# Modulation vectors in a three-layer transformer kernel: four blocks of partial sums transposed into one PSUM bank and summed by VectorE, instead of one-column matmuls after each unit

## The chip, the cores and the metric

The kernel runs on one core of one Trainium2 chip. The metric is the device time of one execution in microseconds (us), the median of the runs shown. The profile is of one execution on the same core. TensorE is called PE in the rows, VectorE DVE, ScalarE ACT, GpSimd POOL, SyncE SP.

## What is computed

512 tokens with 1024 channels go through a first block (retention with four heads, dilated attention in three groups, a gated merge, a squared-ReLU feed-forward) and then through two layers of a second block, the first of which also carries 256 context tokens. Every norm is modulated and every branch gated by vectors that depend on a conditioning vector `c` alone:

```python
mod = jax.nn.silu(c) @ w_ada[l] + b_ada[l]          # (1024) @ (1024 x 6144)
sh1, sc1, g1, sh2, sc2, g2 = jnp.split(mod, 6, axis=-1)
h = modulate(rms_norm(x, norm1_g[l]), sh1, sc1)     # h * (1 + scale) + shift
x = x + g1[:, None, :] * token_mixer(h, ...)
h = modulate(rms_norm(x, norm2_g[l]), sh2, sc2)
x = x + g2[:, None, :] * squared_relu_mlp(h, w_ff1[l], w_ff2[l])
# second block, l = 0, 1: the same six vectors from c_2, and six more from c_ctx_2 for the context,
# both times the same matrix ada_w_2[l]
```

The change concerns how `silu(c) @ w_ada` is summed. Each of the three matrices has 1024 rows and 6144 columns, which are 48 blocks ("chunks") of 128 columns.

## The kernel before, in words

**Units.** All large products run in 244 units of up to 256 weight columns. SyncE loads a unit's weights into `raw`, ScalarE copies them to `w_hi` (`hi`), VectorE subtracts to get `w_lo` (`lo`, L1582), and TensorE does three matmuls for each 128 rows (`product`, L539 to L542) in `gemm`. The weights have two buffers, so `hi` and `lo` of unit n+2 can start only when unit n has been multiplied. A unit with 1024 rows is called a long one here, a unit with 512 rows (the second matrix of a feed-forward) a short one. In the layer with context a unit also multiplies the context tokens. A feed-forward is a head of 2 units, a hardware loop of 3 bodies of 12 units (2 long, 4 short, 2 long, 4 short; units 0 to 11 of a body), and a tail of 10 units (2 long, 8 short; units 0 to 9).

**Modulation vectors.** The first 16 chunks of the first matrix are done ahead of everything. The other 128 are spread over the program. For each, GpSimd (`chunk`, L2188) waits for its DMA, multiplies the 128x1024 block by the vector (L2195), adds eight slices to four, two and one (L2197, L2199, L2201) and leaves a 128x128 block of partial sums in `ada_acc`: its columns have still to be summed over the 128 partitions. The 96 chunks of the second block's matrices are done for two vectors, one after the other, since `c_2` and `c_ctx_2` meet the same weights. After that GpSimd issues the DMA for the chunk after next (L2186). `ada_acc` has two halves, and `ada_raw` two buffers.

**One step for each chunk.** `ada_mm_step` (L663) on TensorE waits until GpSimd has summed the chunk (`ada_sum`) and until VectorE has read the chunk before (`ada_evac`), and multiplies `ada_acc` by a column of ones: one matmul of one column for a one-vector chunk, two for a two-vector chunk. VectorE adds the bias and writes the result to `mod1` (L1625) or `mod2` (L1635). GpSimd may start chunk a when chunk a-2 has been multiplied. In the retention heads eight steps are written out for each head; elsewhere the table `ADA` says how many steps stand behind each unit, in `ada_steps` on TensorE and `ada_outs` on VectorE. The three engines run through the program in their written order, so a step that isn't ready stops TensorE there, and a VectorE instruction that waits for a step stops the `lo` of later units behind it.

## Time and profile before

| | us |
|---|---|
| median of 3 runs (lowest, highest) | 3363.69 (3362.53, 3374.6) |
| the profiled execution, span | 3362.5 |
| TensorE busy in it | 3102.6 (92%) |
| VectorE busy | 1717.3 (51%) |
| ScalarE busy | 1180.7 (35%) |
| GpSimd busy | 1340.9 (40%) |

The span runs from the first to the last instruction, and the median lies 1.2 us above it. Start times below count from the span's start. Busy shares are means over the whole program; what a place waits for is read from the idle time in brackets in the timeline.

### The profile page before, as it was taken

What the parts mean: (1) busy time and instruction counts of PE and PEld (TensorE: products, weight loads), DVE (VectorE), ACT (ScalarE), POOL (GpSimd) and SP (SyncE); (2) the same over time, 40 slices, a digit from 0 to 9 for tenths busy, and PEclk for the clock granted to TensorE, in tenths of its full rate; (3) what the DMA queues carried; (4) which work ended last, traced back from release to release, by engine and by line L of the source; (5) the groups of instructions that cost most, each with busy time, mean ns of one, the idle gap of its engine ahead of it and who ended that gap; (6) DMA issues with size and microseconds to landing.
All of it is one profiled execution on the core that took longest, in us unless ns stands there. A gap on an engine that the chain in (4) does not pass through costs nothing.

```text
span 3362.5 us, 42485 instructions
## 1 busy us (share of the span) xinstructions
PE 3102.6 (92%) x16079; PEld 2615.0 (78%) x16079; DVE 1717.3 (51%) x1792; ACT 1180.7 (35%) x1683; POOL 1340.9 (40%) x1044
## 2 busy tenths in 40 slices
PE   5799999999999899989988899999999988989998
PEld 4677777798987688868977778887887878868886
DVE  4563464424146766763177457655554437544444
ACT  2232233213133333343245433322324326434433
POOL 2445336753536677734610056777770000000000
PEclk7899999999999899999998999999999999999999
DMA  7333332433323334432230022322222221013331
GB/s 264 113 113 97 115 106 94 141 96 94 100 65 125 92 116 125 131 95 69 82 82 1 13 76 63 101 88 89 88 88 70 75 73 28 26 57 97 97 100 63
DMA packets 257779, 303.30 MB, mean 90 GB/s; under 512 B 23340, under 2 KB 229564, under 8 KB 257629
## 3 DMA queue, kind: packets, MB, share of 16 engines
q1 hardware_dynamic: 234716, 224.43, 21.5%
q0 software_dynamic: 19456, 72.00, 7.1%
q10 hardware_dynamic: 3456, 4.72, 0.5%
q8 instruction: 112, 1.84, 0.2%
q14 instruction: 39, 0.31, 0.0%
HBM read 291.95 MB, written 9.18 MB: 90 GB/s over the span
## 4 chain that ended last, share of the span: by engine, by line
PE 31%; POOLq 31%; issue 27%; DVE 4%; DVEq 1%; POOL 1%; SPq 1%; ACT 1%; DMA 0%; ACTq 0%
POOLq L2196 12%; POOLq L2198 9%; PE psum L540 9%; PE psum L541 8%; PE psum L542 8%; POOLq L2200 6%; POOLq L2204 4%; POOL ada_raw L2186 1%; PE psum L873 1%; PE psum L713 1%; DVE w_lo L1582 1%; PE psum L883 1%; SPq L431 1%; PE psum L619 1%; PE psum L698 1%
## 5 line engine op out<-in xcount | busy, mean ns | idle before, releaser
L2195 POOL TENSOR_TENSOR ada_prod<-ada_raw,csil 128x1024 f32<-128x1024 f32 x224 | 453.7, 2026 | 777.8 <-PE psum L669 757.6
L540 PE MATMUL psum<-hs_hi,w_hi 128*128 128x512 f32 x1632 | 653.7, 401 | 60.9 <-DVE hs_lo L1574 35.4
L1582 DVE TENSOR_TENSOR w_lo<-raw,w_hi 128x2048 fp32r<-128x2048 f32 (+1 forms) x244 | 536.9, 2200 | 315.1 <-ACT w_hi L1062 246.6
L541 PE MATMUL psum<-hs_hi,w_lo 128*128 128x512 f32 x1632 | 644.2, 395 | 0.0
L542 PE MATMUL psum<-hs_lo,w_hi 128*128 128x512 f32 x1632 | 643.6, 394 | 0.0
L2197 POOL TENSOR_TENSOR ada_prod<-ada_prod 128x512 f32<-128x512 f32 x224 | 372.0, 1661 | 195.0 <-issue 181.2
L540 PEld LDWEIGHTS psum<-hs_hi,w_hi 128*128 128x128 f32 x1632 | 312.3, 191 | 130.4 <-issue 44.0
L542 PEld LDWEIGHTS psum<-hs_lo,w_hi 128*128 128x128 f32 x1632 | 311.7, 191 | 67.4
L541 PEld LDWEIGHTS psum<-hs_hi,w_lo 128*128 128x128 f32 x1632 | 312.6, 192 | 63.1
L540 PE MATMUL psum<-mid_hi,w_hi 128*128 128x512 f32 x768 | 303.0, 395 | 5.5 <-DVE w_lo L1582 5.4
L542 PE MATMUL psum<-mid_lo,w_hi 128*128 128x512 f32 x768 | 299.4, 390 | 0.0
L541 PE MATMUL psum<-mid_hi,w_lo 128*128 128x512 f32 x768 | 298.9, 389 | 0.0
L1841 DVE TENSOR_TENSOR X<-X,y_t 128x512 f32<-128x512 f32 x208 | 202.3, 983 | 167.1 <-ACT y_t L1324 166.9
L1825 DVE TENSOR_TENSOR r_t<-r_t 128x512 f32<-128x512 f32 x112 | 122.8, 1099 | 313.3 <-ACT r_t L1307 313.2
L1324 ACT ACTIVATE y_t<-psum,mod 128x512 f32<-128x512 f32 x208 | 143.0, 690 | 335.4 <-PE psum L542 315.1
L2199 POOL TENSOR_TENSOR ada_prod<-ada_prod 128x256 f32<-128x256 f32 x224 | 237.1, 1059 | 31.9
L1307 ACT ACTIVATE r_t<-psum 128x512 f32<-128x512 f32 x112 | 66.9, 598 | 450.8 <-PE psum L542 447.2
L540 PE MATMUL psum<-w_hi,hs_hi 128*128 128x256 f32 x704 | 214.8, 305 | 0.0
L541 PE MATMUL psum<-w_hi,hs_lo 128*128 128x256 f32 x704 | 213.7, 304 | 0.0
L542 PE MATMUL psum<-w_lo,hs_hi 128*128 128x256 f32 x704 | 213.7, 303 | 0.0
L1070 ACT CAST w_hi<-raw 128x2048 fp32r<-128x2048 f32 (+1 forms) x138 | 190.6, 1381 | 0.0
L1062 ACT CAST w_hi<-raw 128x2048 fp32r<-128x2048 f32 (+1 forms) x106 | 174.4, 1645 | 13.3 <-issue 8.9
(330 smaller groups left out, 5728.6 us busy)
## 6 DMA issues: line engine op xcount, KB each, us to landing
raw<-in_w_in SPq DMA_DIRECT2D x56, 1024.0 KB, 5.1
ada_raw<-in_ada_w POOLq DMA_DIRECT2D x96, 512.0 KB, 4.7
raw<-in_w_ff SPq DMA_DIRECT2D x48, 1024.0 KB, 5.5
raw<-in_w_ff SPq DMA_DIRECT2D x96, 512.0 KB, 3.4
ada_raw<-in_w_ada POOLq DMA_DIRECT2D x32, 512.0 KB, 4.6
raw<-in_w_in SPq DMA_DIRECT2D x24, 512.0 KB, 5.1
ada<-in_w_ada SPq DMA_DIRECT2D x4, 2048.0 KB, 23.9
raw<-in_w_ret_out SPq DMA_DIRECT2D x16, 512.0 KB, 3.4
```

What stands on the lines that cost most here:

```text
L540: pe.matmul(dst, lhi, rhi, start=start, stop=False)
L541: pe.matmul(dst, llo, rhi, start=False, stop=False)
L542: return pe.matmul(dst, lhi, rlo, start=False, stop=stop)
L1070: act.copy(w_hi[n0_ % 2][:, 0:kt], raw[n0_ % 2][:, 0:kt]).then_inc(hi_done, 1)
L1582: dve.tensor_tensor(w_lo[par][:, 0:kt], raw[par][:, 0:kt], w_hi[par][:, 0:kt].bitcast(F32), ALU.subtract).then_inc(lo_done, 1)
L1841: dve.tensor_tensor(X[:, q, :], X[:, q, :], y_t[r_][:], ALU.add).then_inc(y_free, 1)
L2195: pool.tensor_tensor(ada_prod[:], ada_raw[par][:], bass.AP(c_.tensor, c_.offset, [*c_.ap, [0, P]]), ALU.mult)
L2196: pool.drain()
L2197: pool.tensor_tensor(ada_prod[:, 0:4], ada_prod[:, 0:4], ada_prod[:, 4:8], ALU.add)
L2198: pool.drain()
L2199: pool.tensor_tensor(ada_prod[:, 0:2], ada_prod[:, 0:2], ada_prod[:, 2:4], ALU.add)
L2200: pool.drain()
```

## The change

Four blocks of partial sums now make a set: four one-vector chunks, or two two-vector chunks. `ada_acc` has two halves of four blocks. TensorE does one **turn** for each set (`ada_turn`): four transposes of 128x128 into the four quarters of one PSUM bank, where the sum over partitions has become a sum along the free dimension. VectorE reduces the whole bank to four columns (`ada_red`) with one `tensor_reduce` and adds the bias, with one instruction for the first matrix and two for the others. There are 56 turns (8 + 48), where there were 128 steps. GpSimd computes the same blocks in the same order with the same instructions and DMAs, but waits once for each set: set s starts when turn s-2 is done. In the heads two turns for each head are left, behind the second unit and at the head's end; the table `ADA` is written anew, so that in the tail of the feed-forward with context (`ff_tail_0`) there are now five turns, behind units 1, 3, 5, 7 and 9, and none at the end of its loop body. Some buffers move to make room, and `gn_rstd` becomes the same memory as `gn_std`.

```diff
-ADA = {"gate_a": [1, 1, 0, 1], "ret_out": [0, 1, 0, 0], "att0": [1, 1, 1, 1, 0, 1, 1, 1, 0], "att1": [1, 1, 1, 1, 0, 1, 1, 1, 0],
-       "gate_b": [1, 1, 0, 1], "att_out": [0, 1, 0, 0], "w_o": [1, 1, 1, 1],
-       "ff_head": [1, 1], "ff_body": [1, 0, 0, 1, 0, 1, 0, 1, 0, 1, 0, 1], "ff_tail": [1, 0, 0, 0, 1, 0, 0, 0, 0, 0],
-       "w_in_0": [1] * 9, "w_out_0": [1] * 4, "ff_head_0": [1, 1], "ff_body_0": [1, 1, 0, 1, 1, 1, 1, 1, 0, 1, 1, 1],
-       "ff_tail_0": [1, 0, 1, 0, 1, 0, 0, 0, 0, 0]}
+ADA = {"gate_a": [0, 1, 0, 1], "ret_out": [0, 0, 0, 1], "att0": [0, 1, 0, 1, 0, 1, 0, 1, 0], "att1": [0, 1, 0, 1, 0, 1, 0, 1, 0],
+       "gate_b": [0, 1, 0, 1], "att_out": [0, 0, 0, 1], "w_o": [0, 1, 0, 1],
+       "ff_head": [0, 0], "ff_body": [0, 1, 0, 0, 0, 0, 0, 1, 0, 0, 0, 0], "ff_tail": [0, 1, 0, 0, 0, 1, 0, 0, 0, 0],
+       "w_in_0": [0, 1, 0, 1, 0, 1, 0, 1, 0], "w_out_0": [0, 1, 0, 1], "ff_head_0": [0, 1],
+       "ff_body_0": [0, 1, 0, 0, 1, 0, 0, 1, 0, 0, 1, 0], "ff_tail_0": [0, 1, 0, 1, 0, 1, 0, 1, 0, 1]}
...
-            def ada_mm_step(a, vecs=1, bank_=C1):
+            def ada_turn(a, bank_=C1):
 
                 pe.wait_ge(ada_sum, a + 1)
                 if not (isinstance(a, int) and a == 0):
                     pe.wait_ge(ada_evac, a)
-                for v in range(vecs):
-                    mm = pe.matmul(bank_[:, v:v + 1], ada_acc[:, ada_par[0], v, :], ones_c[:, 0:1], start=True, stop=True)
+                for s_ in range(4):
+                    mm = pe.transpose(bank_[:, s_ * P:(s_ + 1) * P], ada_acc[:, ada_par[0], s_, :], ident[:])
                 ada_par[0] ^= 1
                 mm.then_inc(ada_mm, 1)
...
                 gemm(n, 0, hs_hi, hs_lo, ready=(hs_ready, lambda k: k + 1) if first else None)
-                ada_mm_step(8 * h)
                 gemm(n + 1, 1, hs_hi, hs_lo)
-                ada_mm_step(8 * h + 1)
+                ada_turn(2 * h)
...
-                ada_mm_step(8 * h + 2)
-                ada_mm_step(8 * h + 3)
                 gemm(n + 3, 1, hs_hi, hs_lo, tokens=tile_tok)
...
-                ada_mm_step(8 * h + 4)
-                ada_mm_step(8 * h + 5)
                 gemm(n + 4, 0, hs_hi, hs_lo)
...
-                ada_mm_step(8 * h + 6)
                 gemm(n + 5, 1, hs_hi, hs_lo)
...
-                ada_mm_step(8 * h + 7)
+                ada_turn(2 * h + 1)
...
             def ada_out(a):
 
                 dve.wait_ge(ada_mm, a + 1)
-                dve.tensor_tensor(mod1[:, bass.ds(16 + a, 1)], C1[:, 0:1], vec1[:, bass.ds(24 + a, 1)],
-                                  ALU.add).then_inc(ada_evac, 1)
+                dve.tensor_reduce(ada_red[:], C1[:].rearrange("p (s n) -> p s n", s=4), AX.X, ALU.add).then_inc(ada_evac, 1)
+                dve.drain()
+                dve.tensor_tensor(mod1[:, bass.ds(16 + 4 * a, 4)], ada_red[:], vec1[:, bass.ds(24 + 4 * a, 4)], ALU.add)
...
-                    j_ = a - (80 if l else 32)
-                    dve.tensor_scalar(mod2[l][:, :, bass.ds(j_, 1)], bank_[:, 0:2].rearrange("p (v o) -> p v o", o=1),
-                                      vec2[:, l, bass.ds(j_, 1)], None, ALU.add).then_inc(ada_evac, 1)
+                    dve.tensor_reduce(ada_red[:], bank_[:].rearrange("p (s n) -> p s n", s=4), AX.X, ALU.add).then_inc(ada_evac, 1)
+                    dve.drain()
+                    for c in range(2):
+                        j_ = 2 * (a - ADA_SETS - 24 * l) + c
+                        dve.tensor_scalar(mod2[l][:, :, bass.ds(j_, 1)], ada_red[:, 2 * c:2 * c + 2].rearrange("p (v o) -> p v o", o=1),
+                                          vec2[:, l, bass.ds(j_, 1)], None, ALU.add)
...
+            def sets_of_two(l, i, more=True):
+
+                for half in range(2):
+                    for k in range(2):
+                        chunk(k, 256 + 384 * l + 32 * i + 16 * half + 16, half, 2 * k, (0, 1),
+                              ADA_SETS - 1 + 24 * l + 2 * i + half if k == 0 else None, k == 1)
+                        if half == 0 or more:
+                            load_ada(wada2[l], 2 + 4 * i + 2 * half + k, k)
+                        elif l == 0:
+                            load_ada(wada2[1], k, k)
```

Three places show what moves. First TensorE at the end of the loop body of the feed-forward with context (`midc` and `hc` are the context's activations, `mid` and `hs` the tokens'). Before:

```order
L542 MATMUL psum<-midc_lo_138,w_hi_51 128x256
L665 REGISTER_ALU
L669 MATMUL psum<-ones_c,ada_acc 128x1 x2
L835 REGISTER_ALU
L835 COMPARE_AND_BRANCH
L540 MATMUL psum<-hs_hi,w_hi_52 128x512
```

And now:

```order
L545 MATMUL psum<-midc_hi_136,w_lo_53 128x256
L546 MATMUL psum<-midc_lo_138,w_hi_51 128x256
L833 REGISTER_ALU
L833 COMPARE_AND_BRANCH
L544 MATMUL psum<-hs_hi,w_hi_52 128x512
```

The step at the body's end is gone, and the last matmul of unit 11 stands directly ahead of the loop's branch and of unit 0 of the next body.

Second VectorE in a retention head, between the second weight-column unit and the rotation (`z_lo` is the low part of the head before, `w_lo` the low part of a unit's weights). Before:

```order
L1582 TENSOR_TENSOR w_lo_53<-raw_49,w_hi_51 128x1024
L1654 TENSOR_TENSOR z_lo<-ro,z_hi 128x2048
L1624 REGISTER_ALU
L1625 ISA
L1625 TENSOR_TENSOR mod_60<-psum,vec_59 128x1
L1581 REGISTER_ALU
L1582 TENSOR_TENSOR w_lo_54<-raw_50,w_hi_52 128x1024
```

And now:

```order
L1580 TENSOR_TENSOR w_lo_53<-raw_49,w_hi_51 128x1024
L1656 TENSOR_TENSOR z_lo<-ro,z_hi 128x2048
L1622 ISA
L1623 TENSOR_REDUCE ada_red<-psum 128x4
L1625 ISA
L1625 REGISTER_ALU
L1625 TENSOR_TENSOR mod_60<-ada_red,vec_59 128x4
L1579 REGISTER_ALU
L1580 TENSOR_TENSOR w_lo_54<-raw_50,w_hi_52 128x1024
```

A reduction and an addition of four columns stand where one addition of one column stood, ahead of the `w_lo` of a later unit; the other addition, ahead of the first `w_lo`, is gone.

Third VectorE at the end of the tail with context, where layer 1 of the second block begins (`scale` is its first scale vector, X and CX the residuals, `w_lo` of 2048 elements the units of layer 1). Before:

```order
L1841 TENSOR_TENSOR X<-X,y_t_142 128x512
L1841 TENSOR_TENSOR X<-X,y_t_143 128x512
L1844 TENSOR_TENSOR CX<-CX,y_t_144 128x512
L1582 TENSOR_TENSOR w_lo_54<-raw_50,w_hi_52 128x2048
L1841 TENSOR_TENSOR X<-X,y_t_142 128x512
L1841 TENSOR_TENSOR X<-X,y_t_143 128x512
L1844 TENSOR_TENSOR CX<-CX,y_t_144 128x512
L1909 SCALAR_TENSOR_TENSOR scale_73<-mod_1_72,vec_69 128x8 x2
L1582 TENSOR_TENSOR w_lo_53<-raw_49,w_hi_51 128x2048
```

And now:

```order
L1837 TENSOR_TENSOR X<-X,y_t_142 128x512
L1837 TENSOR_TENSOR X<-X,y_t_143 128x512
L1840 TENSOR_TENSOR CX<-CX,y_t_144 128x512
L1580 TENSOR_TENSOR w_lo_54<-raw_50,w_hi_52 128x2048
L1837 TENSOR_TENSOR X<-X,y_t_142 128x512
L1837 TENSOR_TENSOR X<-X,y_t_143 128x512
L1840 TENSOR_TENSOR CX<-CX,y_t_144 128x512
L1633 TENSOR_REDUCE ada_red<-psum 128x4
L1637 TENSOR_SCALAR mod_1_72<-ada_red,vec_69 128x2 x2
L1905 SCALAR_TENSOR_TENSOR scale_73<-mod_1_72,vec_69 128x8 x2
L1580 TENSOR_TENSOR w_lo_53<-raw_49,w_hi_51 128x2048
```

The residuals of units 8 and 9 had no modulation work behind them; now the reduction of the last turn stands between the last residual and the scales of the next layer.

## Rows read from the trace of the kernel before

**Rows 1.** The page of before, part 1: busy us, share of the span, instructions.

```profile
PE 3102.6 (92%) x16079; PEld 2615.0 (78%) x16079; DVE 1717.3 (51%) x1792; ACT 1180.7 (35%) x1683; POOL 1340.9 (40%) x1044
```

**Rows 2.** Line 669 from 2045 to 2592 us: idle time of PE and its weight loads before it.

```profile
  POOL ada_acc L2201: 30.8, 6
```

**Rows 3.** Timeline of PE at the first and last of three body ends: start, length, [idle].

```profile
2189.70 1.01 PE L669 MATMUL psum<-ones_c,ada_acc 128*128 128x1 f32 x4 [5.07 <-POOL ada_acc L2201]
2193.41 0.79 PE L540 MATMUL psum<-hs_hi,w_hi 128*128 128x512 f32 x1 [2.69 <-issue]
...
2487.21 0.95 PE L669 MATMUL psum<-ones_c,ada_acc 128*128 128x1 f32 x4 [5.02 <-POOL ada_acc L2201]
2488.02 0.77 PE L540 MATMUL psum<-hs_hi,w_hi 128*128 128x512 f32 x1
```

**Rows 4.** Windows behind those three waits: busy us, PEclk eighth.

```profile
2193.00:2203.00 10.00, 9.59 (x35) 7.78 (x35) 3.16 (x2) 0.60 (x1) 7.43 (x7) 0.79 0.26 90
2342.00:2352.00 10.00, 10.00 (x34) 7.95 (x34) 2.75 (x2) 0.60 (x1) 6.85 (x7) 0.73 0.20 65
2488.00:2498.00 10.00, 10.00 (x32) 7.99 (x33) 5.36 (x3) 0.60 (x1) 7.58 (x7) 0.69 0.35 105
```

**Rows 5.** GpSimd: its DMA issues from 2100 on, and parts of one chunk of two vectors.

```profile
L2186 POOL DMA_DIRECT2D ada_raw<-in_ada_w x27: 912/915/924, 2112.9 to 2501.5; - x27
...
2149.31 1.28 POOL L2197 TENSOR_TENSOR ada_prod<-ada_prod 128x512 f32<-128x512 f32 x1 [1.76 <-issue]
...
2158.62 0.73 POOL L2201 TENSOR_TENSOR ada_acc<-ada_prod 128x128 f32<-128x128 f32 x1
2160.17 0.92 POOL L2186 DMA_DIRECT2D ada_raw<-in_ada_w  x1 [0.82 <-issue]
```

**Rows 6.** Timeline of PE: a two-vector step, and four transposes (L923).

```profile
1695.19 0.60 PE L923 MATMUL psum<-ident,ws 128*128 128x128 f32 x4
1695.62 1.45 PE L931 MATMUL psum<-dft,u_f 128*128 128x512 f32 x3
...
2228.93 0.28 PE L542 MATMUL psum<-hc_lo,w_hi 128*128 128x256 f32 x1
2229.05 0.50 PE L669 MATMUL psum<-ones_c,ada_acc 128*128 128x1 f32 x4
2229.42 0.47 PE L540 MATMUL psum<-mid_hi,w_hi 128*128 128x512 f32 x1
```

**Rows 7.** One pair of steps in a retention head, and the waits of all eight.

```profile
142.78 0.28 PE L669 MATMUL psum<-ones_c,ada_acc 128*128 128x1 f32 x2
143.82 0.35 PE L669 MATMUL psum<-ones_c,ada_acc 128*128 128x1 f32 x2 [0.76 <-DVE mod L1625]
144.04 0.36 PE L540 MATMUL psum<-w_hi,hs_hi 128*128 128x256 f32 x1
...
  DVE mod L1625: 4.8, 8
```

**Rows 8.** Groups of VectorE by form: a reduction from PSUM, and the evacuation of a two-vector step.

```profile
L1635 DVE TENSOR_SCALAR mod<-psum,vec 128x2 f32<-128x2 f32 x48 | 10.4, 217 | 247.7 <-PE psum L669 247.7
...
L2006 DVE TENSOR_REDUCE dneg<-psum 128x2 f32<-128x512 f32 x8 | 5.5, 682 | 0.0
```

**Rows 9.** Timeline of VectorE in head 2: the same subtraction, twice.

```profile
335.25 1.23 DVE L1582 TENSOR_TENSOR w_lo<-raw,w_hi 128x1024 fp32r<-128x1024 f32 x1 [2.85 <-ACT w_hi L1070]
...
338.66 2.85 DVE L1582 TENSOR_TENSOR w_lo<-raw,w_hi 128x1024 fp32r<-128x1024 f32 x1
```

**Rows 10.** Waits of PE, heads 1 to 3 (first) and first feed-forward: us, times, longest.

```profile
PE psum L540 <- DVE w_lo L1582: 6.6, 3, 2.2
...
PE psum L540 <- DVE w_lo L1582: 5.7, 6, 1.5
```

**Rows 11.** The last eight units with context: window, and PE at their end.

```profile
2524.60:2592.30 67.70, 67.70 (x395) 59.99 (x393) 29.96 (x37) 27.53 (x42) 2.05 (x3) 1.00 0.25 78
...
2594.01 6.41 PE L619 MATMUL psum<-n_sq,mean_dm 128*128 128x512 f32 x13 [1.45 <-ACT n_sq L1102]
```

More of the change, by code:

```diff
@@ L101, in ada_starts @@
 def ada_starts():
-    start, a = {}, 32
+    start, a = {}, ADA_SETS
     for name in ADA:
@@ L2186, in load_ada, with chunk @@
                 pool.dma_start(ada_raw[par][:], w[:, :, bass.ds(chunk * P, P)]).then_inc(ada_in[par], 16)
-            def chunk(a, par, count, cond=(csil,), first=False):
+            def chunk(par, count, half, slot, cond=(csil,), free=None, last=False):
                 pool.wait_ge(ada_in[par], count)
-                if not first:
-                    pool.wait_ge(ada_mm, a - 1)
+                if free is not None:
+                    pool.wait_ge(ada_mm, free)
                 for v, c in enumerate(cond):
@@ L2231, in _, with sets_of_four @@
-            for par in range(2):
-                chunk(126 + par, par, 1024, (0, 1))
+            def sets_of_four(first_set, i, free):
+                for half in range(2):
+                    for k in range(4):
+                        chunk(k % 2, 64 * i + 32 * half + 16 * (k // 2) + 16, half, k,
+                              free=(free + half if k == 0 and free is not None else None), last=k == 3)
+                        load_ada(wada, 18 + 8 * i + 4 * half + k, k % 2)
+            sets_of_four(0, 0, None)
@@ new lines, in _ @@
+            with pool.Fori(1, 3) as i:
+                sets_of_four(2 * i, i, 2 * i - 1)
+            pool.wait_ge(v3_done, 1)
+            for half in range(2):
+                for k in range(4):
+                    chunk(k % 2, 192 + 32 * half + 16 * (k // 2) + 16, half, k, free=5 + half if k == 0 else None, last=k == 3)
+                    if half == 0 or k < 2:
+                        load_ada(wada, 42 + 4 * half + k, k % 2)
+                    else:
+                        load_ada(wada2[0], k - 2, k % 2)
@@ new lines, in sets_of_two @@
+            def sets_of_two(l, i, more=True):
+                for half in range(2):
+                    for k in range(2):
[5 more added lines that the diff above has]
+                            load_ada(wada2[1], k, k)
@@ L2235, in constants @@
+            for l in range(2):
+                with pool.Fori(0, 11) as i:
+                    sets_of_two(l, i)
+                sets_of_two(l, 11, False)
 def constants():
```

57 lines of the change are left out of this document (16 added, 41 removed).

## The prediction

> **What bounds the kernel now.** I read the page first: TensorE is busy for 92% of the span, the other engines for half of it or less [rows 1]. So TensorE's own time counts in most places, and an edit elsewhere counts where TensorE waits. Next came the waits of the modulation steps. From 2045 us on, in the feed-forward with context, TensorE and its weight loads stood idle for GpSimd's partial sums, 30.8 us in six entries, which are three waits seen by both [rows 2]. The timeline puts them at the ends of the three loop bodies [rows 3]: 5.07 us idle, then the step, then 2.69 us more before the next body's first matmul ("issue": nothing that the profile shows holds it; it comes after a wait right ahead of the loop's branch). The third wait has no branch back behind it, and no such gap. Behind each wait the windows show a mean granted clock of 0.79, 0.73 and 0.69 for 10 us [rows 4]; TensorE had idled some 5 to 9 us before it fell. Last I read GpSimd: from 2112.9 to 2501.5 us it issued 27 DMAs, one for each chunk, hence one two-vector chunk in 388.6 / 26 = 14.95 us, without a pause for TensorE [rows 5]. A body holds ten chunks, 149.5 us, while TensorE needs about 140 us for it: from 2193.41 to 2487.21, less the 5.02 us of the last wait and 8.8 us of the one between, are two bodies in 280 us [rows 3]. There GpSimd is the bound, and nowhere else for long.
>
> **What the change removes on TensorE.** A two-vector step costs 0.37 us: the matmul behind it starts 0.49 us after the one ahead of it, where 0.12 us is the usual spacing [rows 6]. There are 96. I leave out 13: three at the body ends (counted below), two in the tail (below), and eight which the timeline shows ahead of a wait for something else (weights, or the squares of a norm), where time saved is time waited. 83 x 0.37 = 30.7 us.
>
> A turn is four transposes. The trace has a group of four, 1695.19 to the next start at 1695.62, 0.43 us [rows 6]. From below it could cost 0.35 us (the next start doesn't wait for the end), from above four full lengths one after another, 4 x 0.27 = 1.1 us (0.27 is what the last of the four takes, 0.60 less 3 x 0.11). I take 0.43, the same operation in this kernel. Of the 48 later turns 4 are in the tail and 9 ahead of other waits: 35 x 0.43 = 15.1 us. Net gain 15.6 us.
>
> The Trainium skill, "TensorE: Matmul & The Clock Gate", Part 4, gives about 275 ns for a 128x128 bf16 transpose in a kernel's context. That would be 1.1 us for a turn, and 23 us less gain; the row above speaks for 0.11 us each in a row of four.
>
> **The retention heads.** Twice in each head two steps stand in a row, and the second waits for VectorE to have read the first: the pair at 142.78 costs 1.26 us, 0.76 of it waiting [rows 7]. All eight waits are 4.8 us, and the pairs' own time is 8 x 0.50: 8.8 us, all gone. Single steps and the one turn that isn't ahead of a wait give 0.2 us more. The other turns stand ahead of the wait for the group norm's chain, and cost TensorE nothing while it lasts. Gain 9.0 us.
>
> On VectorE a turn costs a reduction of 512 elements from PSUM, 0.68 us by the nearest row, a drain, and one or two small additions of 0.21 us [rows 8]: 1.0 us in the heads, 1.2 us later, where a step cost 0.2. Most of it lies beside idle time of VectorE. It doesn't behind the second unit of heads 1 to 3: `w_lo` of the coming units is queued behind it, and TensorE already waits three times for `w_lo` there, 6.6 us in all [rows 10]. 3 x 0.8 = 2.4 us lost. Also GpSimd will be ahead by a set of four and work through this stretch, where it now pauses. The same subtraction of 1024 elements took VectorE 1.23 us, and 2.85 us beside a multiplication of GpSimd's [rows 9]. I put 2 us on this (0 to 6). The Trainium skill, "GPSIMD Engine Reference", Key points, names such contention, for VectorE instructions with two SBUF inputs; the reduction, with one from PSUM, would be free of it. Net for the heads +4.6 us.
>
> **The first feed-forward.** The turns now stand behind units 1 and 7 of a body, and the reduction ahead of `w_lo` of unit 3 or 9, behind the squares of the hidden part. TensorE waits for `w_lo` six times in this feed-forward, 5.7 us [rows 10]. Four of the seven such places I count as lengthened by 1.0 us: 4 us lost (0 to 7). A turn moves no DMA queue: SyncE's loads keep their order, GpSimd's its own.
>
> **The body ends with context.** Four sets a body are eight chunks, 120 us against TensorE's 140, and no turn stands at the end. The waits go: 5.07 + 1.01 + 2.69 = 8.8 us, the second alike, the third 5.02 + 0.81 = 5.8 us [rows 3]: 23.4 us. The clock gives back 10 x (0.21 + 0.27 + 0.31) = 7.9 us, of which I take 7.5, since the first window begins 0.4 us before its matmuls [rows 4]. Gain 30.9 us.
>
> **What comes late instead: the tail with context.** The ten chunks that the bodies no longer take must come somewhere, and five turns now stand in the tail, behind units 1, 3, 5, 7 and 9. GpSimd can hold two sets at most, and set s starts when turn s-2 is done. Call the turn behind unit 1 time 0; it frees the half for the third of the five sets. A set's sum is ready 1.7 us before its second chunk's DMA is through (2159.35 to 2161.09) [rows 5], so the third set is ready at 0.8 + 29.9 - 1.7 = 29.0 us, in time for unit 5. The fourth starts at 30.7 and is ready at 58.9 us. TensorE is there earlier: the eight units behind time 0 take 67.7 us with two steps [rows 11], 67.0 without; six of them with two turns 51.1 us. It waits 7.8 us. The fifth set starts at 60.6; its first chunk ends 14.3 us later, its second, with no DMA behind or ahead of it, is ready after another 11.6 to 12 us [rows 5]: 86.9 us. TensorE is there at 59.3 + 16.8 = 76.1 us, and waits 10.8. The tail ends at 87.3 instead of 67.7 us. While TensorE waits VectorE is idle, and GpSimd quicker, 2 us off, and 1 us is hidden by the wait for the squares that stands behind it anyway (1.45 us [rows 11]): 17 us lost. A lower clock behind the first wait costs nothing, since GpSimd ends last. Behind the stopped turns VectorE's `w_lo` is held up as well, but TensorE needs it later. If a chunk takes 13.5 us, 9 us are lost; if 16, 23.
>
> **The sum.** 30.9 + 15.6 + 4.6 - 4 - 17 = 30.1 us gained, from the profile's span of 3362.5: 3332.4. The median of the runs is 1.2 us over it: 3334 us. A gain or loss of 0.5%, 17 us, is about what a measurement can tell from no change.
>
> **The rivals.**
> - *The tail costs little* (0.17): GpSimd, beside a VectorE with less to do, needs 13.5 us for a chunk. 8 us less lost, and the small losses in heads and feed-forward halve: 3322.
> - *VectorE holds up the units* (0.18): the reductions and GpSimd's steadier work lengthen waits for `w_lo` in the heads, behind the first gates, and at all seven places of the first feed-forward, or GpSimd is late once more in the dilated attention, where two chunks stand against two units. 12 us more lost: 3346. For it speaks that TensorE waits for `w_lo` already [rows 10], against it VectorE's 51% [rows 1].
> - *The transposes don't overlap* (0.05): 1.1 us a turn, 0.67 x 35 = 23 us: 3357.
> - *The other side, slower* (0.07): every turn stops VectorE's queue, for the evacuation has to wait for TensorE and then takes 1.2 us, and `hi` and `lo` of the next unit can't start before the last is multiplied. If 49 turns more than those counted pass 1.0 us each to TensorE, 49 us are lost and the time is 3383; it decides from 0.6 us each, where the gain is gone. Against it: behind a long unit with context VectorE has some 17 us for 3 us of work.
> - *The change doesn't do what it says* (0.03): GpSimd, with a chunk over 17.5 us, is the bound in the bodies still, and the waits move from their ends to units 1, 4, 7 and 10: about 3362.
>
> The forecast has 0.50, with a range of its own of 3327 to 3341. The likeliest is 3334. For 8 in 10 I cut the other side, the transposes, the lost change, and little below the cheap tail: 3319 to 3350. Faster by over 0.5% (below 3347): 0.50 + 0.17 + 0.12 of the held-up case = 0.79. Within: 0.06 + 0.05 + 0.03 = 0.14. Slower: 0.07.
>
> **What would show it.** The steps: 56 groups of four transposes, 0.43 us from start to start. The bodies: no wait for `ada_acc` in them, granted clock 1.00 at their start, 140 us each. The tail: two waits of TensorE for `ada_acc`, 6 to 11 us each, behind units 7 and 9. The heads: no wait for `mod`, and about 1 us more before the third short unit of heads 1 to 3. VectorE: a reduction of 0.68 us. I am wrong if the tail's waits are missing or double, if GpSimd's chunk moves far from 15 us, or if waits for `w_lo` grow by more than 10 us in all.

## The result, and the profile after it

The changed kernel takes 3417.76 us (median of 4 runs, 3413.49 to 3420.41), the kernel before on the same chip 3365.49 (4 runs). The ratio is 1.0151, with a 95% interval of 1.0136 to 1.0166: 1.5% slower. The forecast was 3334 us, so it missed by 84 us, and by sign.

The profiled execution took 3415.81 us, its span is 3413.7. This is the line of busy times on its page, to be set beside [rows 1]:

```profile
PE 3098.5 (91%) x15855; PEld 2581.5 (76%) x15855; DVE 1818.6 (53%) x1824; ACT 1180.5 (35%) x1683; POOL 1345.4 (39%) x1044
```

TensorE is busy for only 4 us less, where the light kernels below, a pair without most of GpSimd's arithmetic, differ by 24.5 us (3071.8 and 3047.3). Most of the other 20 us is a lower granted clock: its mean is 0.954 of full speed against 0.958 before, and 0.4% of 3100 us is 13 us (an estimate). In the light kernels it is 0.969 and 0.970. GpSimd has the same work. VectorE has 101 us more. The waits of TensorE over the whole span (us in all, times, longest) say what that does:

```profile
PE psum L544 <- DVE w_lo L1580: 79.8, 29, 9.1
PE psum L544 <- DVE hs_lo L1572: 44.0, 15, 11.1
...
PE psum L673 <- POOL ada_acc L2197: 12.4, 2, 7.3
```

In the kernel before the same view has 37.9 us in 20 waits for `w_lo`, 35.4 in 6 for `hs_lo` and 16.0 in 4 for `ada_acc`. So the waits for GpSimd became fewer, as the change set out to do, and those for VectorE grew by 50 us. The groups of VectorE by form (count, busy us, mean ns) show what is new there:

```profile
L1580 DVE TENSOR_TENSOR w_lo<-raw,w_hi 128x1024 fp32r<-128x1024 f32 x116 | 164.5, 1418 | 38.0 <-ACT w_hi L1060 19.8 <-ACT w_hi L1068 17.9
...
L1633 DVE TENSOR_REDUCE ada_red<-psum 128x4 f32<-128x512 f32 x48 | 32.8, 683 | 155.7 <-PE psum L673 155.7
...
L1637 DVE TENSOR_SCALAR mod<-ada_red,vec 128x2 f32<-128x2 f32 x60 | 31.1, 561 | 2.9
L1637 DVE TENSOR_SCALAR mod<-ada_red,vec 128x2 f32 x36 | 27.0, 791 | 5.7 <-issue 5.7
...
L1625 DVE TENSOR_TENSOR mod<-ada_red,vec 128x4 f32 x6 | 4.5, 744 | 1.9 <-issue 1.9
```

The reduction takes what [rows 8] said, 0.68 us. The small additions do not: in these groups they average 0.56 to 0.79 us in place of 0.22.

**Where the time went.** A table of stages, each from the first matmul of its first unit to that of the next stage, parts the two traces (the last columns are of experiments below). "Context" is the layer with context.

| Stage, us | before | changed | light before | light changed | e14 |
|---|---|---|---|---|---|
| four retention heads | 462.3 | 488.9 | 450.1 | 437.6 | 458.9 |
| gate_a, ret_out | 77.0 | 77.0 | 67.4 | 67.3 | 73.4 |
| attention, both passes | 332.3 | 335.4 | 328.9 | 326.8 | 336.4 |
| gate_b, att_out, w_o | 145.9 | 143.8 | 130.6 | 129.7 | 144.6 |
| first feed-forward | 408.7 | 445.8 | 398.1 | 398.4 | 402.1 |
| context, from its input projection to the first loop body | 528.0 | 522.6 | 526.7 | 519.9 | 530.5 |
| context, loop bodies | 442.2 | 416.9 | 420.1 | 414.7 | 415.3 |
| context, tail and the norm behind it | 122.4 | 137.9 | 119.6 | 119.8 | 119.7 |

The bodies with context give 25.3 us, and the tail behind them takes back 15.5. But the heads lose 26.6 us and the first feed-forward 37.1. Those two stages are the whole difference of sign.

**One loss, close up.** The loop of the first feed-forward has six places of one kind: behind its first matrix (units 0 and 1, or 6 and 7), where unit 3 (or 9) waits for `w_lo`. From the first matmul of unit 2 or 8 to that of the next unit, the six took 5.6 to 7.1 us before and take 9.4 or 9.5 now, every time. In the timeline of VectorE and GpSimd at one of them (start, length, instruction, [idle before <- released by]) unit 7 ends at 1342.0:

```profile
1342.85 2.30 DVE L1821 TENSOR_TENSOR r_t<-r_t 128x512 f32<-128x512 f32 x1 [4.71 <-ACT r_t L1305]
1345.08 2.92 DVE L1825 TENSOR_TENSOR mid_lo<-r_t,mid_hi 128x512 fp32r<-128x512 f32 x2
1347.93 0.68 DVE L1633 TENSOR_REDUCE ada_red<-psum 128x4 f32<-128x512 f32 x1
1348.84 1.74 DVE L1637 TENSOR_SCALAR mod<-ada_red,vec 128x2 f32 x2 [0.23 <-issue]
1350.49 1.21 DVE L1580 TENSOR_TENSOR w_lo<-raw,w_hi 128x1024 fp32r<-128x1024 f32 x1
```

And GpSimd at the place one half body earlier, where the turn behind unit 1 ends at 1290.7:

```profile
1290.78 1.89 POOL L2191 TENSOR_TENSOR ada_prod<-ada_raw,csil 128x1024 f32<-128x1024 f32 x1 [19.86 <-PE psum L673]
...
1294.52 1.01 POOL L2195 TENSOR_TENSOR ada_prod<-ada_prod 128x256 f32<-128x256 f32 x1
```

The reader is to see two things. GpSimd had nothing to do for 19.86 us and was released by the transposes. From there it works for some 30 us on end, and the first microseconds of that burst are exactly those in which VectorE must square `r_t`, form `mid_lo`, empty the bank and form `w_lo`. That chain takes 8.85 us from 1342.85 to 1351.70. A turn is placed at the end of a unit, the end of a unit is where VectorE's chain begins, and so GpSimd's burst meets it each time: the square takes 2.30 to 2.38 us at all six places. In the kernel before, whose GpSimd paused for 4 us at most there and so met the chain at chance moments, it takes 0.69, 0.97, 0.99, 1.05, 1.25 and 2.20.

**The clock adds to it.** The six places are 18.3 us of the 37.1, and the one of the same kind in the tail (9.3 in place of 5.4 us) 3.9. The windows of the whole stage (length, then busy us of PE, PEld, DVE, ACT and POOL, then the mean granted clock), before, changed, and in the run e9 below, show how the 37 us divide:

```profile
1109.00:1518.00 409.00, 389.91 (x1689) 310.22 (x1690) 281.94 (x227) 163.36 (x219) 263.77 (x200) 0.98 0.36 112
...
1137.00:1583.00 446.00, 401.37 (x1634) 311.91 (x1635) 282.13 (x229) 163.32 (x219) 220.96 (x163) 0.95 0.32 98
...
1139.00:1549.00 410.00, 385.42 (x1634) 302.13 (x1635) 272.95 (x236) 163.38 (x219) 219.59 (x164) 0.99 0.35 107
```

TensorE stands idle (length less busy) for 44.6 us in place of 19.1, and is busy for 11.5 us more with 55 instructions fewer, since its mean granted clock fell from 0.98 to 0.95. In e9, where the long waits are gone, it is idle for 24.6 us, and the same 1634 instructions take 385.4 us at 0.99. In the heads the clock falls from 0.97 to 0.94, and TensorE's idle time grows from 29.6 to 52.1 us.

### The profile page after: what moved, and what is told of

Its sections match the earlier page's. It is cut to its first block, busy times and chain, and to the rows that moved or that the text cites. A ratio compares the mean times of both kernels' runs of the same rounds, so it can differ in the third digit from the quotient of the medians.

```text
span 3413.7 us, 41761 instructions
## 1 busy us (share of the span) xinstructions
PE 3098.5 (91%) x15855; PEld 2581.5 (76%) x15855; DVE 1818.6 (53%) x1824; ACT 1180.5 (35%) x1683; POOL 1345.4 (39%) x1044
## 3 DMA queue, kind: packets, MB, share of 16 engines
q1 hardware_dynamic: 234716, 224.43, 21.2%
## 4 chain that ended last, share of the span: by engine, by line
PE 47%; issue 20%; POOLq 16%; DVE 8%; DVEq 4%; ACT 2%; SPq 1%; POOL 1%; DMA 0%; ACTq 0%
PE psum L544 13%; PE psum L545 13%; PE psum L546 13%; POOLq L2192 6%; POOLq L2194 5%; POOLq L2196 3%; POOLq L2200 2%; DVE w_lo L1580 2%; PE psum L871 1%; PE psum L714 1%; DVE n_t L1568 1%; PE psum L623 1%; POOL ada_raw L2182 1%; PE psum L881 1%; PE psum L701 1%
## 5 line engine op out<-in xcount | busy, mean ns | idle before, releaser
L1580 DVE TENSOR_TENSOR w_lo<-raw,w_hi 128x2048 fp32r<-128x2048 f32 (+1 forms) x244 | 485.4, 1989 | 439.6 <-ACT w_hi L1060 324.9
L544 PE MATMUL psum<-mid_hi,w_hi 128*128 128x512 f32 x768 | 311.2, 405 | 33.3 <-DVE w_lo L1580 30.0
L1837 DVE TENSOR_TENSOR X<-X,y_t 128x512 f32<-128x512 f32 x208 | 224.1, 1091 | 172.1 <-ACT y_t L1322 171.8
L545 PE MATMUL psum<-mid_hi,w_lo 128*128 128x512 f32 x768 | 306.9, 400 | 0.0
L544 PEld LDWEIGHTS psum<-mid_hi,w_hi 128*128 128x128 f32 x768 | 148.2, 193 | 68.8 <-issue 24.7
L1068 ACT CAST w_hi<-raw 128x2048 fp32r<-128x2048 f32 (+1 forms) x138 | 190.6, 1381 | 0.0
```

What stands on the lines that cost most here:

```text
L544: pe.matmul(dst, lhi, rhi, start=start, stop=False)
L545: pe.matmul(dst, llo, rhi, start=False, stop=False)
L1068: act.copy(w_hi[n0_ % 2][:, 0:kt], raw[n0_ % 2][:, 0:kt]).then_inc(hi_done, 1)
L1580: dve.tensor_tensor(w_lo[par][:, 0:kt], raw[par][:, 0:kt], w_hi[par][:, 0:kt].bitcast(F32), ALU.subtract).then_inc(lo_done, 1)
L1837: dve.tensor_tensor(X[:, q, :], X[:, q, :], y_t[r_][:], ALU.add).then_inc(y_free, 1)
```

## The experiments

Two theories stood against each other. **Theory A**: what stands ahead of `w_lo` in VectorE's order (reduction, drain, additions) holds TensorE up. **Theory B**: GpSimd's partial sums, now made in bursts that start at a turn, slow VectorE where it is late anyway. The kernel before, run beside each group of experiments, had medians of 3365 to 3368 us; where two runs below are compared, their ratios to it are.

### The same GpSimd, nearly without work (e1, e2)

Both kernels lose the same three instructions of each chunk, the multiplication and the first two additions, so that their vectors are no longer the sums. The changed kernel's edit (without the drains between; the other is the same):

```diff
-pool.tensor_tensor(ada_prod[:], ada_raw[par][:], bass.AP(c_.tensor, c_.offset, [*c_.ap, [0, P]]), ALU.mult)
-pool.tensor_tensor(ada_prod[:, 0:4], ada_prod[:, 0:4], ada_prod[:, 4:8], ALU.add)
-pool.tensor_tensor(ada_prod[:, 0:2], ada_prod[:, 0:2], ada_prod[:, 2:4], ALU.add)
-done = pool.tensor_tensor(ada_acc[...], ada_prod[:, 0], ada_prod[:, 1], ALU.add)
+done = pool.tensor_tensor(ada_acc[...], ada_raw[par][:, 0], ada_raw[par][:, 1], ALU.add)
```

> The kernel before, with the multiplication and the first two additions of every chunk on GpSimd left out (its last addition reads two slices of the loaded chunk, so the modulation vectors are not the reference's). Both theories expect it faster than the kernel before: its six waits for GpSimd (30.8 us) go, and VectorE's long additions and subtractions beside GpSimd shorten. Estimate 3280 to 3320 us. It is the mate of the next run.

Measured: 3289.25 us, ratio 0.9774 (0.9753 to 0.9794).

> The changed kernel with the same GpSimd instructions left out. Theory B (GpSimd's work, now in bursts that start at a turn, slows what VectorE does between a gemm's end and the next w_lo, and that is what the forecast missed): without it the change is worth what the forecast gave it apart from waits for GpSimd, 10 to 30 us faster than the light kernel before. Theory A (the reduction, drain and additions ahead of w_lo in VectorE's order hold TensorE up whatever GpSimd does, 1.0 to 1.2 us at most of the 56 turns): 10 to 30 us slower than the light kernel before.

Measured: 3257.44 us, ratio 0.9678 (0.9653 to 0.9702). So with GpSimd nearly silent the change is a gain of 31.8 us, where it is a loss of 52 with it. Theory B expected 10 to 30. Theory A expected a loss here as well, and is out as the main cause: the reductions and additions stand in the same places. GpSimd's arithmetic costs the kernel before 76 us (22 of them in the context's bodies, whose ends wait for it [rows 3]), and the changed one 160.

The group of VectorE's small additions in the light changed kernel shows what their length depended on:

```profile
L1637 DVE TENSOR_SCALAR mod<-ada_red,vec 128x2 f32<-128x2 f32 x60 | 14.2, 282 | 2.9
L1637 DVE TENSOR_SCALAR mod<-ada_red,vec 128x2 f32 x36 | 7.1, 229 | 5.7 <-issue 5.7
```

### No small additions, and the reduction behind w_lo (e3, e5)

```diff
-dve.tensor_reduce(ada_red[:], bank_[:].rearrange("p (s n) -> p s n", s=4), AX.X, ALU.add).then_inc(ada_evac, 1)
-dve.drain()
-for c in range(2):
-    dve.tensor_scalar(mod2[l][:, :, bass.ds(j_, 1)], ada_red[...], vec2[...], None, ALU.add)
+dst = mod2[l][:, :, bass.ds(2 * (a - ADA_SETS - 24 * l), 2)].rearrange("p v c -> p c v")
+dve.tensor_reduce(dst, bank_[:].rearrange("p (c v n) -> p c v n", c=2, v=2), AX.X, ALU.add).then_inc(ada_evac, 1)
...
+dve.tensor_tensor(mod2[l][:], mod2[l][:], <biases of the layer, for both vectors>, ALU.add)
```

> The changed kernel in which the reduction writes the vectors' columns themselves and the biases are added in three bulk additions before use, so that the 104 small additions and 56 drains are gone; reductions, turns and GpSimd as they are. The additions took 70.3 us in the changed kernel's profile where 0.22 each would be 23. Theory A: most of that stands ahead of a w_lo that TensorE waits for, so 25 to 45 us faster than the changed kernel (3373 to 3393). Theory B (large instructions slowed by GpSimd are the loss): 10 us or less.

Measured: 3402.87 us, ratio 1.0113 (1.0096 to 1.0130), against 1.0151 of the changed kernel: 13 us faster. That is above what B allowed and half of A's least.

The second kernel collects the evacuations in a list that `lo` empties behind its own instruction:

```diff
+pend.append(lambda: ada_outs_now(name, k, i))
...
 dve.tensor_tensor(w_lo[par][:, 0:kt], raw[par][:, 0:kt], w_hi[par][:, 0:kt].bitcast(F32), ALU.subtract).then_inc(lo_done, 1)
+flush()
```

> The run with direct reductions, in which moreover the reduction of nearly all turns (all but the last of each head and those of the context layer's projections, first two units and tail) stands behind the next w_lo in VectorE's order, not ahead of it. To be set against the run with direct reductions alone (3402.87). Theory A (what stands ahead of w_lo is the loss): 0.7 us at some 35 turns, 20 to 30 us faster than that run. Theory B (GpSimd's bursts are the loss): at most 10 us faster.

Measured: 3391.4 us, ratio 1.0055 (1.0029 to 1.0082), with a wide spread (3371.73 to 3403.82, 7 runs): 20 us below e3 by the ratios, 11.5 by the medians: more than B's 10 either way, and at the low end of A's 20 to 30 by the ratios. By the stages the first feed-forward falls from 435 to 414 us, and the heads rise from 482 to 492. At the six places a unit takes 7.2 us, where it took 7.5 to 9.3 in e3, 8.7 in the mean: 1.5 us for a reduction of 0.68. Order on VectorE is part of the loss, then, where a burst meets the chain. Why it counts for twice the reduction's length isn't shown.

The same move on the changed kernel with its small additions left in (e4) gave no time: the next reduction would have written `ada_red` without waiting for the addition that still reads it. A expected 30 to 50 us of it, B 10 or less.

### The turns moved away from the chain (e6)

```diff
-"ff_body": [0, 1, 0, 0, 0, 0, 0, 1, 0, 0, 0, 0]
+"ff_body": [0, 0, 0, 1, 0, 0, 0, 0, 0, 1, 0, 0]
```

> The changed kernel with the six turns of the first feed-forward's loop moved from behind units 1 and 7 of each 12 (the second unit of a first matrix) to behind units 3 and 9; nothing else. A set takes GpSimd some 30 us from its turn on, so it then works during the last units of a second matrix and the first unit of the next, and is done when TensorE waits for mid_lo and w_lo at the start of the second matrix. Theory B: most of the six losses of 4 to 5.6 us at units 2 to 4 and 8 to 10 goes, 15 to 28 us faster than the changed kernel (3390 to 3403). Theory A: same turns, same reductions ahead of a w_lo, within 5 us of the changed kernel.

Measured: 3379.21 us (10 runs), ratio 1.0040 (1.0025 to 1.0055): 37 us faster than the changed kernel, more than the 15 to 28 expected. The first feed-forward falls from 445.8 to 407.5 us. The other stages move by some 8 us or less, which is about what they scatter by: the heads, whose code is all but the same there, took 482, 486 and 492 us in e6, e8 and e9. Theory A, as it was put, is wrong here. But the move takes two things out of the chain at once, the reduction and the start of the burst.

### The burst held, the reduction left (e9)

```diff
-pool.wait_ge(ada_mm, free)
+pool.wait_ge(ada_go, free)
...
 residual(n + j, j, nr, sec)
+if name + str(suffix) == "ff_body" and j == 1:
+    dve.memset(go_t[:], 0.0).then_inc(ada_go, 1)
```

> The changed kernel with its turns and reductions where they are, but in the first feed-forward's loop GpSimd may start the next set only when VectorE has finished the residual additions of unit 3 (or 9), two units after the turn, told by a new semaphore that a one-element memset of VectorE raises there (elsewhere the last small addition of a turn raises it). It parts the place of the reduction from the start of the burst, which moved together when the turns were moved. Theory B (the burst's start): most of the 38 us that moving the turns gave, so 20 to 38 us faster than the changed kernel (3380 to 3398). Theory A (the reduction ahead of w_lo where VectorE is late already): within 6 us of the changed kernel.

Measured: 3381.83 us (10 runs), ratio 1.0052 (1.0037 to 1.0067): 33 us faster by the ratios and 36 by the medians, with every reduction where the change had put it. The first feed-forward takes 409.0 us, as in the kernel before (408.7), and TensorE's waits for `w_lo` in it, 5.7 us before and 28.6 in the changed kernel, are 6.9. The six places take 5.6 us each, and the square 0.69 at all of them. VectorE's timeline at the same place as above:

```profile
1328.96 0.69 DVE L1826 TENSOR_TENSOR r_t<-r_t 128x512 f32<-128x512 f32 x1 [4.22 <-ACT r_t L1307]
1329.57 1.46 DVE L1830 TENSOR_TENSOR mid_lo<-r_t,mid_hi 128x512 fp32r<-128x512 f32 x2
1330.95 0.68 DVE L1636 TENSOR_REDUCE ada_red<-psum 128x4 f32<-128x512 f32 x1
1331.87 0.37 DVE L1640 TENSOR_SCALAR mod<-ada_red,vec 128x2 f32 x2 [0.23 <-issue]
1332.14 1.22 DVE L1582 TENSOR_TENSOR w_lo<-raw,w_hi 128x1024 fp32r<-128x1024 f32 x1
```

The same five steps take 4.40 us in place of 8.85, and the reduction and its additions 1.2 us of them. GpSimd starts when it is told to, after the residual additions of unit 9, with 16.70 us of idle time ahead:

```profile
1341.38 1.89 POOL L2198 TENSOR_TENSOR ada_prod<-ada_raw,csil 128x1024 f32<-128x1024 f32 x1 [16.70 <-DVE go_t L1858]
```

This is the run that settles the first feed-forward: the loss comes from the start of the burst. The reduction alone makes none, though beside a burst its place counts (e5).

### The heads and the tail (e7, e8)

```diff
                 gemm(n + 1, 1, hs_hi, hs_lo)
-                ada_turn(2 * h)
...
                         mm.then_inc(s_done, 1)
+                ada_turn(2 * h)
...
-                              free=(free + half if k == 0 and free is not None else None), last=k == 3)
+                              free=(free + half if k == 0 and free is not None else 1 if k == 0 and half else None), last=k == 3)
```

The second part holds GpSimd's second set of all until the first turn.

> The changed kernel with the first turn of each head moved from behind the second unit to behind the scores (ahead of the second value unit, where the kernel before had its third step), and GpSimd's second set of all held until the first turn. Its 30 us burst then lies beside the long second value unit and not beside the four short units of the previous head's output product. Theory B: the losses at those units (7.5 us in each of three heads) and at the start (7.8 and 6.6) mostly go, 15 to 35 us faster than the changed kernel. Theory A: within 5 us of it.

Measured: 3401.1 us, ratio 1.0083 (1.0054 to 1.0112): 17 us at the low end of B's range by the medians, 23 by the ratios. In its profile the heads take 472.2 us (488.9 in the changed kernel), but the short units of heads 1 to 3 are helped unevenly. The third of them starts 14.0, 11.7 and 9.1 us after the second (12.5, 13.0 and 13.3 in the changed kernel, 7.8 each time before).

```diff
-"w_in_0": [0, 1, 0, 1, 0, 1, 0, 1, 0], "w_out_0": [0, 1, 0, 1], "ff_tail_0": [0, 1, 0, 1, 0, 1, 0, 1, 0, 1]
+"w_in_0": [0, 1, 0, 1, 0, 1, 0, 1, 1], "w_out_0": [1, 1, 0, 1], "ff_tail_0": [0, 1, 0, 0, 0, 1, 0, 0, 0, 1]
```

> The changed kernel with another distribution of the last 12 turns but those of the loop: 5 turns in the context layer's input projection instead of 4, 3 in its output projection instead of 2, 1 in the first two feed-forward units as before, 3 in the tail instead of 5. GpSimd then has its sets ready at the tail. Both theories: the two waits of 12.4 us in all go, and the last bursts no longer reach into the next layer's first units (8.9 us lost there); 10 to 20 us faster than the changed kernel (3398 to 3408).

The run also drains VectorE ahead of each of these reductions. Measured: 3410.81 us, ratio 1.0126 (1.0099 to 1.0153): 7 us by the medians and 8 by the ratios, short of the 10 to 20 expected. In the profile no wait for `ada_acc` is left, and the tail's stage falls from 137.9 to 121.1 us. That is 17 us, of which the medians show less than half. The rest isn't traced: TensorE's waits for `w_lo`, over the whole program, are 89.9 us in this profile against 79.8.

### All together (e10, e11)

The list of places with the moves of e6, e7, e8 and the direct reductions of e3; in attention, gate_b, att_out and w_o the turns stand one unit or so earlier:

```diff
+"att0": [0, 1, 0, 1, 1, 0, 1, 0, 0], "gate_b": [1, 0, 1, 0], "att_out": [0, 1, 0, 0], "w_o": [1, 0, 1, 0],
+"ff_tail": [0, 0, 0, 1, 0, 1, 0, 0, 0, 0]
```

> All that helped, together: direct reductions, first turn of a head behind the scores and the hold at the start, loop turns of the first feed-forward behind units 3 and 9, its tail's behind 3 and 5, the context layer's distribution of the run with a new plan, and in attention, gate_b, att_out and w_o each stage's last turn one unit or so earlier (units 1, 3, 4, 6; 0, 2; 1; 0, 2). If the gains of the single runs add up (38, 17, 15 and 7 us of 3418): 3341, range 3325 to 3360, so faster than the kernel before. If they are the same time counted twice: 3365 or more.

Measured: 3348.45 us (7 runs), ratio 0.9951 (0.9935 to 0.9968). By the medians the four runs' gains are 77 us, and 69 of them are here, together with whatever the turns moved in the other stages are worth, which have no run of their own. The kernel is 0.5% faster than before.

> The same with the reductions moreover behind the next w_lo (all but the last of each head and those of the context layer outside its loop). Deferring gave 11 us on top of direct reductions where the bursts lay badly. Theory A: 8 to 15 us faster than the run without it. Theory B: with the bursts out of the way 0 to 5 us, since VectorE then has slack at the turns.

Measured: 3352.35 us (8 runs), ratio 0.9954 (0.9935 to 0.9972): no gain over e10, so not the 8 to 15 us of A, and at the lower edge of B's 0 to 5. Once no burst meets it, the reduction ahead of `w_lo` costs nothing that these runs can tell; each ratio is known to 6 us.

### GpSimd paced in the heads (e12, e13, e14)

```diff
+def pace(i, c):
+    if isinstance(i, int) and i == 0:
+        return (None, None, 3, 4, 5, 5, 6, 6)[c]
+    return 10 * i + (-3, -2, -1, 0, 5, 5, 6, 6)[c]
...
+if pace is not None:
+    pool.wait_ge(lo_done, pace)
```

> The changed kernel with the first turn of each head behind the scores, and in the four heads GpSimd's eight chunks a head started one by one where the kernel before started them (each waits for the w_lo that follows the unit behind which the old step stood), in place of bursts of four. Turns, transposes and reductions stay as in the run with moved head turns (3401.1, its heads 472 us up to the first gate unit; the changed kernel 489, the kernel before 462; the two light kernels 450 and 438). Theory B (it is the burst's shape and place, not its amount): the heads fall to 450 to 460, the whole to 3380 to 3392. Theory A: the heads stay at 472 within 4 us, since the same reductions stand in the same places.

Measured: 3399.33 us, ratio 1.0095 (1.0075 to 1.0114). The heads did fall to 455.7 us in the profile, inside B's 450 to 460. The whole did not follow: it misses B's 3380 to 3392, 2 us under e7 by the medians and 4 over it by the ratios. Its profile has new waits behind the heads, from 560 to 720 us:

```profile
PE psum L673 <- POOL ada_acc L2204: 15.3, 4, 6.3
```

> The run with everything that helped (3348.45, its heads 470 us) with the same pacing of the chunks in the heads. Theory B: 12 to 20 us off the heads, 3328 to 3340, near what the forecast gave the change (3334). Theory A: 3345 to 3352.

Measured: 3346.95 us, ratio 0.9934 (0.9917 to 0.9950). The whole lies in A's range and misses B's 3328 to 3340, while the heads do what B said: 456.9 us against e10's 470.1. Behind them stand the same kind of waits, 20.6 us in 5, in that stretch against 5.9 us in 2. A GpSimd that is held back in the heads no longer has its sets ready where the sets of two vectors begin. The last run drops the pacing for the fourth head's second set:

```diff
-pace=pace(3, 4 * half + k))
+pace=pace(3, k) if half == 0 else None)
```

> The placed and paced run (3346.95, its heads 457 us) with the pacing of the last set of the fourth head left out, so that GpSimd is ahead again when the sets of two vectors begin. In that run TensorE then waited five times for GpSimd between 597 and 713 us, 20.6 us in all, against two waits of 5.9 us in the placed run without pacing. Theory B: the heads stay within 3 us of 457 and those waits fall to 6 to 10 us, so 3333 to 3340 in all. If it stays at 3345 or more with the waits gone, the heads' gain is lost elsewhere and something beyond the bursts and the waits is at work.

Measured: 3342.18 us (5 runs, 3334.86 to 3344.12), ratio 0.9925 (0.9906 to 0.9943). The waits fell as expected:

```profile
PE psum L669 <- POOL ada_acc L2201: 6.2, 2, 3.4
```

and the heads stayed at 458.9 us. The profiled span is 3333.2 us against e13's 3347.6, so 14.4 us less, which is the length of the waits taken away. The medians differ by 5 only, and the median lies 2 us above the expected range. The profiled execution of e13 was one of its slower ones (3349.29), that of e14 its fastest (3334.86). The two stages behind the heads took 82.2 and 342.0 us in e13 and take 73.4 and 336.4 here. That the waits took the heads' gain is shown by the two traces; how much of it a median run gets back is not settled better than 5 to 14 us. By its median this is the fastest kernel here that leaves nothing out, 0.75% below the kernel before; its interval overlaps that of e13.

## Why the prediction was wrong

Step by step, by its own names.

**The change on TensorE** was right, and a little better than priced. A turn costs 0.36 us from its first transpose to the next matmul, in the median of all 56, where the forecast took 0.43 from [rows 6]:

```profile
1290.09 0.60 PE L673 MATMUL psum<-ident,ada_acc 128*128 128x128 f32 x4
1290.44 0.48 PE L544 MATMUL psum<-mid_hi,w_hi 128*128 128x512 f32 x1
```

The figure of about 0.275 us for one transpose that the Trainium skill gives ("TensorE: Matmul & The Clock Gate", Part 4) is for bf16 and doesn't hold for four of fp32 in a row here, 0.09 us each. The light kernels measure steps, turns and the pairs of the heads together, with no long wait for GpSimd in either: 31.8 us by the medians, 24.6 by the spans. By its own terms the forecast has 15.6 + 9.0 = 24.6 us for them. That the spans give the same to a tenth is chance, since the medians differ by 7 us more.

**The body ends with context** were right. No wait for `ada_acc` is left in the three bodies, and windows of 10 us at the starts of the second and third body and of the tail show the granted clock that the forecast named, where [rows 4] had 0.79, 0.73 and 0.69:

```profile
2244.00:2254.00 10.00, 9.17 (x40) 7.58 (x41) 4.39 (x3) 2.33 (x2) 8.68 (x7) 1.00 0.24 71
2384.00:2394.00 10.00, 9.45 (x41) 7.81 (x42) 4.09 (x3) 1.96 (x2) 8.79 (x6) 1.00 0.25 69
2521.00:2531.00 10.00, 10.00 (x51) 8.43 (x50) 8.69 (x5) 3.24 (x4) 9.29 (x6) 1.00 0.28 77
```

From the start of a body's last unit to the start of the second unit behind it the changed kernel gained 9.1, 9.9 and 9.3 us on the kernel before: 28.3 us of the 30.9. Inside the bodies the forecast's prices for steps and turns (27 x 0.37 - 12 x 0.43) give 4.8 us, and 0.4 came: units 2 and 8 take 9.7 us in every body, where five of the six took 8.4 before, and 8.4 in the light changed kernel. So contention took a little here too.

**The tail with context** was right in kind, and near in size. The two waits stand behind units 7 and 9, as forecast, with 5.15 and 7.28 us in place of 7.8 and 10.8:

```profile
2613.25 1.11 PE L673 MATMUL psum<-ident,ada_acc 128*128 128x128 f32 x4 [5.15 <-POOL ada_acc L2197]
...
2640.35 1.11 PE L673 MATMUL psum<-ident,ada_acc 128*128 128x128 f32 x4 [7.28 <-POOL ada_acc L2197]
```

With the norm behind them the stage lost 15.5 us of the 17 forecast. That this is nearer than the waits, 12.4 us in place of 18.6, is partly luck: the stage's mean granted clock fell from 0.97 to 0.94, and the forecast had said that a lower clock costs nothing there. e8 takes the waits away.

**The heads** are the first step that failed. The forecast gave them +4.6 us: the removed pairs 9.0, a loss of 2.4 for the reduction, and "GpSimd will be ahead by a set of four and work through this stretch", on which it put 2 us, 0 to 6. They lost 26.6. The light kernels gain 12.5 us there, so what GpSimd takes is 39 us (26.6 + 12.5), not 2. The mechanism was seen, with the right row ([rows 9], 1.23 against 2.85 us), and sized by one instruction. It can act on any of the instructions that VectorE runs beside a burst. In head 1 of the changed kernel five of the twelve instructions of the rotation take longer than the 0.68 us of the other seven, these two most, and the `w_lo` behind it comes 2.29 us long, ahead of the third short unit:

```profile
233.84 3.02 DVE L1664 TENSOR_TENSOR rope_t<-qk_raw,rope 128x512 f32<-128x512 f32 x1
...
245.04 2.59 DVE L1670 TENSOR_TENSOR qk_rot<-qk_rot,rope_t 128x512 f32<-128x512 f32 x1
...
249.01 2.29 DVE L1580 TENSOR_TENSOR w_lo<-raw,w_hi 128x1024 fp32r<-128x1024 f32 x1
```

Nor did the forecast see the start: the first two sets wait for no turn, so GpSimd makes eight chunks in a row beside the first `hs_lo`, and the second unit comes 8.2 us later than before (29.4 against 21.2 us after the first). It is the third and fourth chunk that matter most: with the fifth held until the first turn (e7) it still comes after 27.5, with the third and fourth held as well (e12) after 19.8. With the turn moved and the chunks paced the heads take 455.7 us, 33 of the 39 back.

**The first feed-forward** is the second step that failed, and the larger. The forecast had 4 us lost there (0 to 7), at 1.0 us for each of four places of seven, and gave it also some of the removed steps. The stage lost 37.1 us. The 1.0 us of VectorE's own time was about right (1.2 us in the held run, and no loss in it). What it left out is the release: it counted a turn as work for TensorE and VectorE, and asked of GpSimd only whether its sum is ready in time. It didn't ask when GpSimd's next burst begins, which the turn decides, nor what VectorE does then. e9 changes that alone, and takes back 33 us. The forecast also had nothing for the lower clock behind the new waits, which is 11.5 us of the 37.1.

**VectorE's price for a turn** had a wrong row for its last term. The 0.21 us for a small addition came from [rows 8], where the operand lies in PSUM. The new additions read both operands from SBUF. Without GpSimd's arithmetic they take 0.16 to 0.28 us on average by group; with it 0.56 to 0.79, the two in the first head 1.8, and the longest of all 2.4. The 56 reductions from PSUM took 0.675 to 0.693 us, each of them, in the thick of the bursts or not. The Trainium skill ("GPSIMD Engine Reference", Key points) names contention with VectorE instructions that have two SBUF inputs. The trace agrees, if a per-partition scalar read from SBUF counts as such an input, which that section doesn't say. The forecast cited it for the reduction and overlooked that it speaks against the additions. Removing them, with their drains, gave 13 us (e3).

**The rivals.** "VectorE holds up the units" named the right waits and the right places and priced them at 12 us more than the forecast, where heads and first feed-forward came out 64 us worse than forecast (31.2 and 33.1). "The other side, slower" had the right sign, with 3383 us of the 3418, by the wrong mechanism: it charged each turn to VectorE's queue, in every stage. The light kernels and e11 show that this costs nothing measurable where no burst lies beside it, and e5 that it costs 11.5 to 20 us where one does. The forecast's own warning, that it is wrong "if waits for `w_lo` grow by more than 10 us in all", is what happened: they grew by 41.9 us, those for `hs_lo` by 8.6.

What stays open: the last kernel (e14) still loses 21.3 us in the heads, 9.6 in the attention and 14.9 in gate_b, att_out and w_o against the light changed kernel (the kernel before loses 12.2, 3.4 and 15.3 against its own). Whether a finer pacing, or partial sums of another shape, gets that back wasn't tried.

## What to carry to other kernels

When a change makes a helper engine's work coarser, its amount stays but its phase changes. Ask of each release what it starts, how long that lasts, and what the engine that it slows is doing at that moment. A step at the end of a unit starts the burst at the beginning of the other engine's critical chain. Here the same bursts two units later cost 33 us less.

Price contention by the whole chain that lies beside the burst, not by one lengthened instruction. One run of each kernel with the helper's arithmetic cut out tells how much of a result is contention. Waits that are added to a busy TensorE can cost more than their length: here 25.5 us of idle time came with 11.5 us of slower matmuls.

## What the runs showed of the hardware

- What VectorE loses beside GpSimd depends little on the size of its instruction in the two that were followed. A multiplication of 128x512 went from 0.69 to 2.30 us, and an addition of 2 elements a partition, both operands in SBUF, from 0.21 to 2.15: it seems to wait until GpSimd's instruction is through (0.5 to 1.9 us for its shapes), then to run. That it waits, rather than runs slower, is only argued from these lengths.
- A reduction of 512 elements from PSUM is untouched: 0.675 to 0.693 us in all 56.
- What the whole pays: GpSimd's arithmetic (1341 us busy less 254 in the light kernel, and 1345 less 290) lengthened VectorE's busy time by 304 us in the kernel before, and by 358 in the changed one. The two sums differ by 54 us, while the time lost differs by 84. The amount isn't what decides: in the first feed-forward the mean square of `r_t` was even shorter in the changed kernel than before (1.06 against 1.42 us from 1150 to 1450 us). It was longer at the six places where TensorE waited for what follows it.
- TensorE's granted clock was lower where it had to wait more. In the first feed-forward the mean was 0.95 of full speed with 44.6 us idle, and 0.98 and 0.99 with 19.1 and 24.6 (before, and e9). Between the changed kernel and e9, 1634 instructions in both, that is 401.4 against 385.4 us of work.
